# Normalising softmax probabilities inside their transposition instead of before it

## The reference, cut to what matters

```python
def attend(q_nope, q_rope, k_nope, k_rope, v):
    s = jnp.einsum('bqhd,bkhd->bhqk', q_nope, k_nope, preferred_element_type=jnp.float32)
    s = s + jnp.einsum('bqhr,bkr->bhqk', q_rope, k_rope, preferred_element_type=jnp.float32)
    p = jax.nn.softmax(s * ATTN_SCALE, axis=-1).astype(v.dtype)
    return jnp.einsum('bhqk,bkhd->bqhd', p, v)
...
    # latent queries see context + latent keys (768); context queries see context keys only (256)
    o_attn = latent_attention(qn, qr, concat([ckn, kn]), concat([ckr, kr]), concat([cv, v]))
    ...
    if update_ctx:                      # layer 0 only
        co_attn = attend(cqn, cqr, ckn, ckr, cv)
```

## Time and profile before

| | |
|---|---|
| median of three runs | 2209.18 us (2206.84 to 2209.38) |
| profiled execution, its time | 2210.52 us |
| profiled execution, its span | 2208.7 us |
| mean granted TensorE clock | 0.991 |
| busy: PE, PEld, DVE, ACT, POOL | 97%, 80%, 55%, 23%, 41% of the span |
| attention stage of layer 0 | 424.2 to 592.8 us |
| attention stage of layer 1 | 1608.7 to 1736.3 us |

### The profile page before, as it was taken

One profiled execution on the slowest core, in us unless ns is written; L12 is line 12 of the kernel. 1 busy time (PEld: TensorE's weight loads), 2 busy tenths in 40 slices (PEclk: granted clock), 3 DMA queues, 4 the chain that ended last, 5 costly groups with the idle time before them and its releaser, 6 DMA issues.

```text
span 2208.7 us, 30382 instructions
## 1 busy us (share of the span) xinstructions
PE 2153.5 (97%) x12388; PEld 1761.0 (80%) x12388; DVE 1222.4 (55%) x1887; ACT 504.8 (23%) x814; POOL 899.7 (41%) x492
## 2 busy tenths in 40 slices
PE   6999999999999999999999999989999999999998
PEld 4888888766688888888888888868866787888886
DVE  6998971455563445454565423694256756353453
ACT  3114121354400220110201111312255312010110
POOL 2441443200143344444444443436320355766663
PEclk8999999999999999999999999999999999999999
DMA  7363364233453432122223254535310443322221
GB/s 277 104 137 95 114 211 124 88 113 116 171 196 125 157 118 88 58 77 86 84 80 103 94 196 184 122 137 193 114 55 12 177 172 109 106 96 97 103 97 67
DMA packets 105390, 267.79 MB, mean 121 GB/s; under 512 B 22650, under 2 KB 42490, under 8 KB 103470
## 3 DMA queue, kind: packets, MB, share of 16 engines
q1 hardware_dynamic: 68928, 190.87, 25.1%
q10 hardware_dynamic: 36334, 75.07, 10.4%
HBM read 227.56 MB, written 37.88 MB: 120 GB/s over the span
## 4 chain that ended last, share of the span: by engine, by line
PE 85%; DVE 11%; ACT 1%; DMA 1%; issue 1%; SPq 0%; POOL 0%; ACTq 0%; DVEq 0%; POOLq 0%
PE ps L463 64%; PE ps L1046 3%; PE ps L918 3%; PE ps L1061 2%; PE ps L1094 2%; PE ps L581 2%; PE ps L472 2%; DVE t_in L2172 2%; DVE t_out L2172 1%; PE ps L956 1%; PE ps L776 1%; PE ps L989 1%; PE ps L478 1%; PE ps L944 1%; DVE ps L1919 1%
## 5 line engine op out<-in xcount | busy, mean ns | idle before, releaser
L1282 POOL TENSOR_SCALAR whi<-raw 128x1024 fp32r<-128x1024 f32 x244 | 272.3, 1116 | 1257.6 <-PE ps L463 702.4
L1285 POOL TENSOR_TENSOR wlo<-raw,whi 128x1024 fp32r<-128x1024 f32 x244 | 627.9, 2574 | 20.4
L463 PE MATMUL ps<-hh,whi 128*128 128x512 f32 (+1 forms) x1560 | 466.9, 356 | 5.3 <-ACT gt L1490 2.5
L463 PE MATMUL ps<-hh,wlo 128*128 128x512 f32 (+1 forms) x1560 | 462.4, 353 | 0.0
L463 PE MATMUL ps<-hl,whi 128*128 128x512 f32 (+1 forms) x1560 | 462.1, 353 | 0.0
L463 PEld LDWEIGHTS ps<-hh,whi 128*128 128x128 f32 x1560 | 254.6, 188 | 49.7 <-ACT gt L1490 2.9
L463 PEld LDWEIGHTS ps<-hl,whi 128*128 128x128 f32 x1560 | 255.0, 188 | 43.4 <-issue 0.2
L463 PEld LDWEIGHTS ps<-hh,wlo 128*128 128x128 f32 x1560 | 254.1, 188 | 42.9
L2105 DVE SCALAR_TENSOR_TENSOR x<-ps,ada,x 128x512 f32<-128x512 f32 x120 | 75.5, 659 | 345.8 <-PE ps L463 345.8
L463 PE MATMUL ps<-midh,whi 128*128 128x512 f32 (+1 forms) x768 | 234.0, 359 | 1.8 <-DVE midl L2135 1.8
L463 PE MATMUL ps<-midh,wlo 128*128 128x512 f32 (+1 forms) x768 | 231.5, 355 | 0.0
(11 more groups left out here) (251 smaller groups left out, 2830.3 us busy)
## 6 DMA issues: line engine op xcount, KB each, us to landing
raw<-in_w_main SPq DMA_DIRECT2D x244, 512.0 KB, 3.3
ada_gap<-in_ada_w SPq DMA_DIRECT2D x40, 512.0 KB, 10.0
ada_mixer<-in_ada_w SPq DMA_DIRECT2D x32, 512.0 KB, 4.0
g_d<-gt ACTq DMA_DIRECT2D x24, 384.0 KB, 2.3
gl<-g_d ACTq DMA_DIRECT2D x8, 1152.0 KB, 5.4
ada_first<-in_ada_w SPq DMA_DIRECT2D x16, 512.0 KB, 15.4
cout_d<-cz SPq DMA_DIRECT2D x12, 512.0 KB, 5.0
cout<-cout_d ACTq DMA_DIRECT2D x6, 1024.0 KB, 8.4
```

Source lines behind the costliest of these rows:

```text
L463: ins = pe.matmul(ps[:, p % 4, a:b], ww[:, w % W_SLOTS, kw * P:(kw + 1) * P], xx[:, kx, a:b], start=(first and i == 0 and j == 0), stop=(l ...
L1282: pool.tensor_scalar(whi[:, u, :], raw[:, u % 2, :], 1.0, 0.0, ALU.mult, ALU.add).then_inc(w_split.sem, 1)
L1285: pool.tensor_tensor(wlo[:, u, :], raw[:, u % 2, :], whi[:, u, :].bitcast(F32), ALU.subtract).then_inc(w_split.sem, 1)
```

## The change

In step 4 the probabilities are no longer multiplied. VectorE multiplies the 128x128 identity by the reciprocal sums instead and writes it to a new tile `inv` of three buffers; this now signals `p_ready`. In step 5 the transposes become ordinary float32 products with stationary `pr` (not normalised) and moving `inv`: the result is the transposed block with each query's column scaled. No wait, no semaphore, no DMA and no place in any engine's order is altered.

```diff
+        inv = rest("inv", 86016, [P, 3, P])
...
                     for c in kb:
-                        ins = pe.transpose(ps[:, 2, c * P:c * P + P], pr[:, u % 3, c * P:c * P + P], ident[:, :])
+                        ins = pe.matmul(ps[:, 2, c * P:c * P + P], pr[:, u % 3, c * P:c * P + P], inv[:, u % 3, :],
+                                        start=True, stop=True, skip_group_check=True)
                     ins.then_inc(pt_done.sem, pt_done.mark((l, h2, u)))
...
                     dve.wait_ge(rsum_ready.sem, rsum_ready.at((l, h2, u)))
-                    a = 0 if b < 4 else 512
-                    dve.tensor_scalar(pr[:, u % 3, a:TOK], pr[:, u % 3, a:TOK], rsm[:, c:c + 1],
-                                                       None, ALU.mult).then_inc(p_ready.sem, p_ready.mark((l, h2, u)))
+                    dve.tensor_scalar(inv[:, u % 3, :], ident[:, :], rsm[:, c:c + 1], None, ALU.mult).then_inc(
+                        p_ready.sem, p_ready.mark((l, h2, u)))
```

## The result

The changed kernel takes 2251.35 us (median of 5, 2250.74 to 2255.05) against 2209.18 us for the kernel before: ratio 1.0194, 95% interval 1.0182 to 1.0205, which is 40 to 45 us slower. The forecast was 2248, from 2238 to 2260.

What follows compares the result with a forecast made beforehand. TensorE, busy 97% of the span and 85% of the chain, was taken as the bound. Second passes +47.1 us, less 2.3, 3.8 and 2.5 given back, made +38.5 us: 2248 us (+1.8%), range 2238 to 2260.

Steps and rivals of the forecast that it cites:

- Two passes: In attention's transposition on TensorE, each float32 product takes two passes of 0.1117 us; together +47.1 us.
- The short VectorE instruction: VectorE's normalisation shrinks to 128x128, 0.29 us: 0.33 us less in a wide unit, 0.07 in a narrow one.
- Starts of a pair: At the start of a pair of heads, unit 0's transposes come 0.33 us sooner, seven times: -2.3 us.
- The bound changes hands in the third pairs: In the third pairs TensorE replaces VectorE's ring as bound, period 2.63 us; gives back 3.8 us.
- Small waits go: In the other pairs' early units, 0.12 us of small waits a unit vanish over some 21 periods: -2.5 us.
- Sum: Over both attention stages, 47.1 - 2.3 - 3.8 - 2.5 = +38.5 us; about 21 and 17 us by stage.
- One pass: Rival: the product with a diagonal tile runs in one pass of 0.110 us on TensorE; 2203 us, chance 0.03.
- Waits worth more: Rival: all 22.6 us that transposes' weight loads waited for the normalisation come back; 2234 us, chance 0.07.
- Ring through ScalarE: Rival: later transposes delay ScalarE's copy and the exponential behind it, wide units taking 3.9 us; 2329 us, chance 0.02.
- Dearer start: Rival: each of the 80 units' products costs 0.1 us more to start, nothing given back; 2264 us, chance 0.06.
- Four times a transpose: Rival: a float32 product on TensorE costs four times a transpose, +137 us less 8.6; 2338 us, chance 0.02.

Runs made afterwards that it cites:

- product twice: The changed kernel with every product of the transposition done twice, the second writing the same again; 2340.47 us, ratio to before 1.0604.
- product alone: The kernel before with its transposes made ordinary float32 products with the plain identity, VectorE still normalising the probabilities first; 2254.46 us, ratio 1.0215.
- VectorE's part alone: The changed kernel with the transposes and plain identity of before, so the result lacks the normalisation; 2201.01 us, ratio to before 0.9974.

## Why the prediction was right

- **Two passes.** Right, and the largest term: 832 records, 1.34 us a block, 0.1117 us a pass (product twice: 92.9 us for 832 passes). The gross cost was put at 47.1 us. On the chain, between the first and the last block of each stage, the transposition holds 54.4 + 44.9 = 99.3 us after and 26.7 + 21.3 = 48.0 before, where 7 of the blocks were off the chain behind VectorE.
- **The short VectorE instruction.** Put at 0.29 us, measured 0.287; its worth alone 4.6 us, measured 4.5.
- **Starts of a pair.** Put at seven, -2.3 us. Against the value products ahead of them the first blocks come 0.27 to 0.34 us sooner in all seven, 2.3 us together. After the change the instruction is on the chain six times (three in each layer), 0.30 us each; at the first pair of layer 1 the chain now comes through a transfer, the gates (DMA g_d, 2.00 us) and ScalarE. That this is nearly all that VectorE's saving gives in the changed kernel is shown by product alone, 3.25 us slower.
- **The bound changes hands in the third pairs.** Right: period 2.63 us in layer 1 and behind the first block only TensorE pieces on the chain, in both layers. In layer 0 the step was mis-sized a little. The starts of the blocks there:

```profile
533.06 1.60 PE L1095 MATMUL ps<-inv,pr 128*128 128x128 f32 x12
...
535.79 1.50 PE L1095 MATMUL ps<-inv,pr 128*128 128x128 f32 x12
...
538.45 1.60 PE L1095 MATMUL ps<-inv,pr 128*128 128x128 f32 x12
...
541.19 1.50 PE L1095 MATMUL ps<-inv,pr 128*128 128x128 f32 x12
```

  Three periods take 8.13 us, not 7.9. The first, 2.73 us, is that of every pair that begins behind VectorE; the other two are 2.70 on average, since the third block waited for VectorE once more. The longer of the two engines' work, 2.63 us, is not the only bound: half of the round through both engines is (5.73 - 0.33) / 2 = 2.70. In layer 1 it is (5.46 - 0.33) / 2 = 2.57 and stays under TensorE's 2.63. Against the trace of before the third pairs cost 0.19 us in layer 0 and 1.11 in layer 1, put at 0 and 1.0.
- **Small waits go.** The other pairs run block, scores, block without a gap, 2.63 us a unit after the first. By the starts of the blocks the 21 periods gave back 2.3 us, put at 2.5.
- **Block starts.** A block that had waited went from 0.88 to 1.60 us, and one behind a mix from 0.81 to 1.53: +0.72 each, where the sum put +0.68 everywhere. In the units behind these first ones, where such blocks stand, the stages grew by 0.8 us more than the sum has; that it is the block starts is argued from the pieces, and no run isolates it.
- **Sum.** Forecast +21 and +17 us in the stages, measured +22.05 and +17.77; given back 47.1 - 39.8 = 7.3 us, put at 8.6. The 1.3 us between are the terms above by the starts of the blocks: 0.3 in the third pairs, 0.2 in the small waits, 0.8 in the later units. The rest of the difference to the median (42.2 against 38.5) lies outside the stages, where the executions differ from one another by more than that.
- **The rivals.** One pass: not taken by the float32 product, though it is what float32r does. Waits worth more: refuted by VectorE's part alone. Ring through ScalarE: not there even with 24 passes. Dearer start: real, 0.04 us in place of 0.1. Four times a transpose: 1.34 against 0.66 us is twice; the measurement decides against the figure of the Trainium skill (TensorE: Matmul & The Clock Gate, Terms) for this shape. The clock stayed at 1.00, so what the same page says of transposes and the clock gate (Part 4: PE-mode transpose) changed nothing here.

## What to carry to other kernels

Before work is moved from one engine to the one that carries the chain, count the records of an operation of the same shape and type in the trace: a float32 transpose is one pass and a float32 product two, and here that difference (47 us) was ten times what relieving the other engine was worth by itself (4.5 us). A wait in the list of waits is not a saving: count how often the instruction stands on the chain and multiply by what it gets shorter. Where two engines wait for each other, the period is not just the larger of their own work: follow the round through both, add its pieces, and divide by the units that it takes in. Here that gave 2.87, 2.73, 2.70 and 2.20 us where the traces have 2.87, 2.73, 2.70 and 2.20; the first was read from its own trace, and the other three are estimates that change only the pieces that differ.

## What the runs showed of the hardware that was not expected

- A float32r product of 128x128 by 128 columns takes 0.103 us a pass, hardly less than a float32 pass (0.1117) or a float32 transpose (0.110), though its 191 ns weight load is that of the float32 pass and the transpose's is 141 ns.
- Two engines at 2.63 and 2.64 us of work a unit gave a period of 2.87 us, at 2.63 and 2.38 us 2.73, at 2.63 and 2.31 us 2.70, and at 1.95 and 2.05 us 2.20.
